# Second block's modulation vectors: 96 weight tiles multiplied on TensorE during the spreading of the gates, instead of 160 row products on VectorE during the expert stage

## The reference, cut to what matters

```python
def modulation(cond, w_mod, b_mod):
    return jnp.split(jax.nn.silu(cond) @ w_mod + b_mod, 6, axis=-1)   # 1024 -> 6 x 1024, for 2 layers, cond = c and c_ctx

def peer(...):                       # first block
    ... idx, gate = the 16 chosen experts of each head and their softmax
    act = gelu(einsum('td,thkd->thk', hb, u_tab[idx])) * gate
    return einsum('thk,thkd->td', act, v_tab[idx])
```

## Time and profile before

| | |
|---|---|
| median of 3 runs | 4271.44 us (4268.54 to 4271.95) |
| profiled execution | 4277.81 us, span of the trace 4276.0 us |
| spreading loop | 1098 to 1289 us of the span |
| expert stage | 1289 to about 2350 us of the span |
| instructions on DVE for this modulation | 160 of 1.22 us |

### The profile page before, as it was taken

How to read it: one execution, slowest core, us unless ns; L and a number is a source line. 1 busy time by engine, 2 the same in 40 slices (tenths; PEclk the granted TensorE clock), 3 DMA queues, 4 the chain that set the end, 5 groups by cost and what they waited for, 6 DMA issues and landing times.

```text
span 4276.0 us, 50001 instructions
## 1 busy us (share of the span) xinstructions
PE 3972.7 (93%) x19979; PEld 3173.8 (74%) x19979; DVE 2581.3 (60%) x4442; ACT 1424.2 (33%) x2405; POOL 1699.5 (40%) x1029
## 2 busy tenths in 40 slices
PE   7888999999778999999999799889999989889998
PEld 4768755448667888888988666778888868656886
DVE  5687655438995899999887436444434430645334
ACT  4212211113683333333333336532222131533222
POOL 3246433124894444434444320033222354444443
PEclk9998999999889999999999899999999989999999
DMA  7110310142237999989997100012122112002331
GB/s 260 65 35 2 118 47 25 64 159 91 107 143 269 332 326 332 333 319 338 358 330 267 63 20 16 16 45 74 60 64 60 55 50 66 9 26 80 97 94 50
DMA packets 191332, 562.86 MB, mean 132 GB/s; under 512 B 16283, under 2 KB 66651, under 8 KB 188540
## 3 DMA queue, kind: packets, MB, share of 16 engines
q1 hardware_dynamic: 151100, 405.83, 27.1%
q0 software_dynamic: 40000, 153.84, 10.2%
HBM read 530.24 MB, written 29.36 MB: 131 GB/s over the span
## 4 chain that ended last, share of the span: by engine, by line
PE 54%; DVE 16%; issue 4%; POOL 4%; ACT 4%; DMA 1%; DVEq 0%; POOLq 0%; ACTq 0%
PE psum L271 14%; PE psum L273 14%; PE psum L272 14%; PE psum L277 11%; DVE pair L261 4%; DVE selrow L1952 3%; DVE junk L1974 2%; POOL o L1858 1%; PE psum L372 1%; DVE tok L1962 1%; DMA selrow<-peerrow,hiU 1%; DVE Al L1943 1%; ACT Ah L2032 1%; POOL Pe L2811 1%; DVE psum L1941 1%
## 5 line engine op out<-in xcount | busy, mean ns | idle before, releaser
L250 POOL TENSOR_TENSOR pair<-raw_ring,pair 128x1024 fp32r<-128x1024 f32 x263 | 645.5, 2461 | 1266.9 <-ACT pair L240 1214.0
L240 ACT CAST pair<-raw_ring 128x1024 fp32r<-128x1024 f32 x502 | 513.6, 1048 | 403.8 <-PE psum L273 369.0
L271 PE MATMUL psum<-pfh,pair 128*128 128x384 f32 (+1 forms) x1152 | 401.2, 348 | 22.4 <-DVE Al L1943 9.6
L273 PE MATMUL psum<-pfh,pair 128*128 128x384 f32 (+1 forms) x1152 | 396.7, 344 | 0.0
L272 PE MATMUL psum<-pfl,pair 128*128 128x384 f32 (+1 forms) x1152 | 396.3, 344 | 0.0
L271 PE MATMUL psum<-ffh,pair 128*128 128x512 f32 (+1 forms) x1056 | 379.8, 360 | 16.9 <-DVE ffl L2173 16.0
L272 PE MATMUL psum<-ffl,pair 128*128 128x512 f32 (+1 forms) x1056 | 379.3, 359 | 0.0
L273 PE MATMUL psum<-ffh,pair 128*128 128x512 f32 (+1 forms) x1056 | 379.3, 359 | 0.0
L2080 POOL DMA_INDIRECT selrow<-peerv,hiU x128 | 238.2, 1861 | 295.0 <-DVE tok L1962 255.5
L2080 POOL DMA_INDIRECT selrow<-peerrow,hiU x128 | 217.0, 1695 | 288.7 <-DVE hiF L1952 263.8
L271 PE MATMUL psum<-pair,Ah 128*128 128x512 f32 x768 | 305.5, 398 | 9.3 <-DVE pair L261 7.6
(11 more groups left out here) (644 smaller groups left out, 9068.7 us busy)
## 6 DMA issues: line engine op xcount, KB each, us to landing
raw_ring<-wmod SPq DMA_DIRECT2D x144, 512.0 KB
raw_ring<-peeru SPq DMA_DIRECT2D x128, 512.0 KB
raw_ring<-peerv SPq DMA_DIRECT2D x128, 512.0 KB
raw_ring<-win SPq DMA_DIRECT2D x48, 512.0 KB
gates<-stage SPq DMA_DIRECT2D x12, 2048.0 KB, 7.2
Gb<-gates SPq DMA_DIRECT2D x32, 768.0 KB, 9.3
raw_ring<-wgate SPq DMA_DIRECT2D x44, 512.0 KB
raw_ring<-wup SPq DMA_DIRECT2D x44, 512.0 KB
```

The costliest lines, as they stand in the source:

```text
L240: ac.e.copy(self.pair(t)[0], k.R.of(t)).then_inc(*k.A.up("hi", t))
L250: po.e.tensor_tensor(lo, k.R.of(t), hi.bitcast(F), ALU.subtract).then_inc(*k.G.up("lo", t))
L271: e.matmul(out, w[0], x[0], start=first, stop=False, skip_group_check=True)
L273: return e.matmul(out, w[1], x[0], start=False, stop=last, skip_group_check=True)
```

## The change

The product is done on PE, in the spreading loop. `w_mod` is laid out untransposed in tiles, so that tile t holds the eight 128-row blocks of 128 output columns. `modulated(t)` multiplies each block (moving, 128 columns) with a stationary 128 x 32 matrix of the conditions, silu(c) and silu(c_ctx) in its first two columns and zeros elsewhere. The eight products go in turn to four column positions of the array, that is to PSUM partitions 0, 32, 64 and 96, each position summing two. When four tiles are in a bank, ACT copies it to SBUF (`copied`), PE multiplies it with a 0/1 matrix `sel4` that adds the four positions and turns the result (`turned`), and ACT copies eight columns into `mods2`. Eight tiles are done ahead of the loop, and tile u+8 after unit u. The spread results now have four PSUM banks instead of six, the modulation two. The ring's order is changed: the 96 `wmod2` tiles stand after U9 (with U10, U11 and U12 between them), and U13 and all that follows stands after them. SP's loads between the gate writes are changed too. `deal()` charges ACT 0.2 more per unit, and so hands 201 `o1` to POOL, 111 to ACT, 72 to DVE. In the expert stage `mods`, the loads of the condition rows and their silu are gone; two additions of the bias stand at its start.

```diff
@@ tensor_route
+    def modulated(t):
+        if t % 4 == 0:
+            B.take(("mod2", t // 4), 1, PAIR)
+            pe.wait_ge(B.free(("mod2", t // 4)), A.at("cond2"))
+        o = slice(128 * (t % 4), 128 * (t % 4) + 128)
+        w = k.R.of(("wmod2", t))
+        pe.wait_ge(k.R.at(("wmod2", t)))
+        for q in range(8):
+            r = slice(32 * (q % 4), 32 * (q % 4) + 32)
+            i = mm(e, B.of(("mod2", t // 4))[r, o], k.cond2[:, q, :], w[:, 128 * q:128 * q + 128], q < 4, q > 3)
+        i.then_inc(*P.up("mod2", t))
+        k.R.over(("wmod2", t), P.now())
+    def turned(g):
+        pe.wait_ge(A.at("mrow2", g), G.at("sel4"))
+        for c in range(4):
+            i = mm(e, B.of(("mod2", g))[:, 2 * c:2 * c + 2], k.mrow2[g % 2][:, 128 * c:128 * c + 128], k.sel4)
+        i.then_inc(*P.up("modT2", g))
+    for t in range(8):
+        modulated(t)
+    turned(0)
+    turned(1)
     choose(0)
     for u in range(SPREADS):
-        bank = B.take(("sp", u), 1, SIX)
+        bank = B.take(("sp", u), 1, FOUR)
...
+        if u + 8 < 96:
+            modulated(u + 8)
+        if u % 4 == 2 and 2 <= (u + 2) // 4 < 24:
+            turned((u + 2) // 4)
@@ deal
-        load["scalar"] += 0.58
+        load["scalar"] += 0.58 + 0.2
@@ scalar_route
+    ac.wait_ge(k.G.at("cond2"))
+    e.activation(k.cond2[:, :, 0:2], v3(k.vec["c2"], 2), AF.Silu).then_inc(*A.up("cond2"))
...
+    def copied(g):
+        ac.wait_ge(P.at("mod2", 4 * g + 3), P.at("modT2", g - 2) if g > 1 else None)
+        e.copy(k.mrow2[g % 2], B.of(("mod2", g))).then_inc(*A.up("mrow2", g))
+    def turned(g):
+        i, j = g // 12, 4 * (g % 12)
+        ac.wait_ge(P.at("modT2", g))
+        e.copy(k.mods2[i][:, j:j + 4, :], v3(B.of(("mod2", g))[:, 0:8], 2)).then_inc(*A.up("modT2", g))
+        B.over(("mod2", g), A.now())
+...
         if u > 1:
             spread(u - 2)
+        if u % 4 == 1 and 2 <= (u + 3) // 4 < 24:
+            copied((u + 3) // 4)
+        if u % 4 == 3 and 2 <= (u + 1) // 4 < 24:
+            turned((u + 1) // 4)
@@ vector_experts
+    for i in range(2):
+        e.tensor_tensor(k.mods2[i], k.mods2[i], bc(...bmod2...), ALU.add).then_inc(*V.up("mods2", i))
-            if 0 <= t - MODS < 98:
-                mods(t - MODS)
@@ sync_program
-    R.load(sp, ("U", FIRST + 7))
     for ch in range(CHUNKS):
+        R.load(sp, ("wmod2", min(8 * ch + 18, 95)))
         sp.wait_ge(A.at("sp", 8 * ch + 7))
         e.dma_start(gd[ch], k.stage[ch % 2]).then_inc(*k.stl[ch % 2].up())
-        if ch == 0:
-            R.load(sp, ("U", AHEAD - 1))
-        if ch == 9:
-            R.load(sp, ("V", 1))
     R.load(sp, ("V", 3))
```

More of the change, by code:

```diff
@@ L1497, in lay_peer @@
     k.Gb = [m.take("Gb", 4 * DENSE) for _ in range(2)]
-    both = m.at
-    k.cb2 = [m.take("crow", 1024) for _ in range(2)]
-    k.junk = m.take("junk", 1024)
-    m.at = both
     k.tok = v3(m.take("tok", 4096), 1024)
@@ L1818, in scalar_route @@
         B.over(("ht", hf), A.now())
+    def copied(g):
[6 more added lines that the diff above has]
+        B.over(("mod2", g), A.now())
+    for g in range(2):
+        copied(g)
+    for g in range(2):
+        turned(g)
     choose(0)
@@ L1860, in pool_route @@
     G.name("end", "route")
-NG, MODS = 64, 16
+NG = 64
 def ups(gi):
@@ L3592, in load_order @@
         use(("wq", n))
-    for n in range(AHEAD):
+    for n in range(FIRST):
+        use(("U", n))
+    for t in range(96):
+        if t - 8 in BESIDE:
+            use(("U", BESIDE[t - 8]))
+        raw(("wmod2", t), d["wmod2"][t])
+    for n in range(FIRST + len(BESIDE), AHEAD):
         use(("U", n))
@@ L3687, in sync_program @@
         if t > 0:
[L3688 to L3691 removed]
+            due = W.when[("U", t + 1)] if t > 113 else [n for v in range(t) for n in W.when[("V", v)]]
+            R.load(sp, due[-1] if due else None)
             sp.wait_ge(V.at("act", t))
```

58 lines of the change are left out of this document (18 added, 40 removed).

## The result

| | before | after |
|---|---|---|
| median | 4269.99 us (4267.96 to 4271.95, 4 runs) | 4324.01 us (4321.00 to 4325.87, 4 runs) |
| ratio | | 1.0122 [1.0108, 1.0136] |
| profiled execution, span | 4277.81, 4276.0 us | 4325.87, 4324.1 us |

The direction was right, and the time lies inside the range of 4260 to 4325, but the forecast of +24 us was less than half of the +54. I split both spans at four marks: the last product of the query scores (`kt,qs`), the first and the last copy of `stage`, the last multiplication by `Al` (the end of the expert stage).

The account below looks back on a forecast made before the run. PE bounds the expert stage; in the loop four engines stand close together. Ahead 1, loop 4 + 24 + 10 = 38, expert stage's start 1, expert stage -16: +24 us, median 4295, range 4260 to 4325.

Parts of the forecast that it names:

- What bounds the kernel, and the expert stage: Expert stage: PE bounds it, with 18.2 us lost beside busy DVE and DMA engines; 16 us come back, bounds 8 and 19.
- The start of the expert stage: Start of the expert stage: six tiles load behind the last gate write, mostly covered; costs 1 us, bounds 0 and 6.
- The price of a tile: Spreading loop, on PE: a tile's 16 passes run four abreast, 0.43 us plus 0.2 for mode changes, 0.63 us.
- The two waits: Spreading loop: PE waits for tiles behind gate writes, 24 us (0 to 47); ACT waits for `turned`, 10 us (0 to 15).
- the loop's engines: Spreading loop: the new division of `o1` and ACT's copies add work to POOL, DVE and ACT; 4 us on the loop.
- the loop would be 215 to 240 us long: Sign in the trace after: the spreading loop takes 215 to 240 us rather than 191.
- Ahead of the loop: Before the spreading loop: ACT's exponential stands behind both groups' copies; costs 1 us, bounds 0 and 3.
- only two column positions: Rival, spreading loop: only two positions run abreast, a tile costs 0.43 us more on PE; 4313 us, chance 0.15.
- none: Rival, spreading loop: no positions run abreast or issue limits, a tile costs 1.9 us on PE; 4338 us, chance 0.07.
- The buffers swallow it: Rival, spreading loop: buffers absorb tile waits and handshake, the loop costs only its engines' 4 us; 4261 us, chance 0.17.
- the case in which it comes out even: Rival between swallowed and forecast, spreading loop: half the waits remain; about 4272 us, chance 0.13.
- the change does not do what it says: Rival, expert stage: its losses were not DVE's or the DMA's, so nothing returns; 4311 us, no chance given.

Follow-up runs that it names:

- e14: The changed kernel with the 16 condition columns loaded into a free stretch of cand, so other buffers lie as in the kernel before; ratio 1.0144.
- e7: The kernel before with the modulation's 160 DVE products out of the expert stage and its 96 loads kept; ratio 0.9947.
- e8: The kernel before with the modulation's 96 loads out of the expert stage and the 160 products kept, made on the condition rows; ratio 0.9999.
- e4: The kernel before with both the modulation's 160 DVE products and its 96 loads out of the expert stage; ratio 0.9963.
- e3: The changed kernel with ACT's small copy one unit later and SP loading four tiles further before each gate write; ratio 1.0039.
- e2: The changed kernel with SP loading tiles up to 8ch+22 instead of 8ch+18 before a gate write; ratio 1.0039.
- e5: e3 with each modulation tile in the loop loading only 128 columns (64 KB), used by all eight products; ratio 1.0019.
- e6: e3 with one product for a tile instead of eight, from the ninth tile on; ratio 1.0037.
- e9: e3 with U8, U9 and U10 three tiles earlier in the order of the ring's loads; ratio 1.0040.
- e17: The kernel before with the turn of the six PSUM banks moved on by three behind the loop; ratio 1.0027.
- e12: The kernel before with 16 unused columns more among the vector constants, so the buffers behind them lie 64 bytes further; ratio 0.9987.

## Why the forecast was half of the result

**What bounds the kernel, and the expert stage: right.** The term was -16 us, bounds 8 and 19. At equal places of the buffers it is -16.4 (e14's 1052.4 us against 1068.8). e7 and e8 show that of the two causes it named (DVE from 93 to 70%, the loads' share) only the first counts. Of the -13.3 us in the trace of after, the other 3 are the 64 bytes; the kernels with the new places and nothing of this work on DVE scatter from 1055.4 to 1058.8. One reading on the way was wrong: from 2000 us on not 56 products were still to come but 29, and only one for each tile (L1974 has ended):

```profile
L1976 DVE CUSTOM_DVE_ANT_0 raw_ring<-raw_ring,crow 128x1024 f32<-128x1024 f32 x29 | 35.3, 1217 | 0.0
```

So the full window there was weaker evidence that the products don't bound PE than it seemed.

**The start of the expert stage: right.** The term was 1 us; e14's expert stage, with six tiles loaded behind the last write, is 0.3 us longer than that of e4, which has neither products nor tiles.

**The price of a tile: right.** 0.63 us forecast, 0.57 measured at the full clock and 0.65 on average, four positions abreast. The Trainium skill ("TensorE: Matmul & The Clock Gate", Part 3) has 2.38 times for three positions. Here 96 passes at four positions took 2.83 us; less the 0.27 us that one pass takes by itself that is 0.027 us from start to start, where the whole array has 0.107 to 0.11: the trace shows some 4 times for four, and no run has three. The drain at a change of mode ("TensorEngine Tiling", Tiling Modes) agrees with 0.57 us in the loop against 0.43 from tile to tile in a row (16 x 0.027).

**The two waits: right in sum, partly by luck.** Terms: 24 us (half of 47) for the tiles and 10 for `turned`, 34 together; e3, with both edits, takes 33.5 us from the loop. The parts did not come as reckoned. PE waited for tiles 30.7 us and not 47, and "I take half" is not what happened: e2 took all but 1.8 us of these waits away and shortened the loop by 30.0, in part through the clock, which the prediction did not price. The wait for `turned` is worth 14.2 us alone and 3.5 once the tile waits are gone. Its term counted 2.6 us of PE's work against 1.9 of ACT's; it left out that in the two units with `turned` and a projection of U another 4.4 us stand ahead, and that each tile wait is handed to ACT through it.

**The step that failed: the loop's engines, "That is 4 us on the loop".** With both waits gone e3's loop is still 25.7 us longer than before. The division of `o1` is right (POOL's work +3.7 us, e3); what was put at nothing are three other things. PE's own work: "PE needs 1.75 us of a unit's 1.99. It fits". The sum prices every pass at the full clock and leaves the three projections of U out; e5 shows up to 1.99 us of PE a unit, and e6, with one product for eight, takes 7.6 us off the loop. The bytes: worked out at "16.2 us for a chunk, against 15.9", and then not added; e5 gives them 10.2 us. And POOL's wait for the rounded U, which comes later when the ring is full of tiles: 12 us in e3, of which an earlier place in the ring (e9) gives 4 back, and 6.8 us of the loop. How the three share the 25.7 us is open, as they overlap and no kernel has all three edits. So the loop was 59 us longer instead of 38, and the sentence that the loop would be 215 to 240 us long was missed by 6.

**Ahead of the loop: 1 us forecast, 3.5 measured**, above the bound of 3. The chain named (tiles 7 and 8, copy, `turned`, exponential) is the one in the trace. e5 shows that it takes the loads to make it late.

**What no step looked at.** Behind the expert stage the prediction had nothing. In fact +11.5 us lie there from the banks (e17), some 9 us come back there from the 64 bytes (e12: -5.5 in all, after +1.0 and +2.3 further ahead), and where the difference would be +2.7 the trace shows -2.2. Single profiles scatter that much there: 1907.9 to 1919.6 us in four kernels that don't differ behind the expert stage (before, e4, e7, e8). The two nearly cancel, so a total alone would have shown neither.

Of the rivals, "only two column positions" (4313) and "none" (4338) fell with the price of a tile. "The buffers swallow it", and the case in which it comes out even, fell with e2; "the change does not do what it says" (4311) fell with e7. That 4324 lies inside the range is luck: its upper part was there for two positions abreast, and what filled it is the engines' term. The upper bounds of both waits would have given 4323, but the waits were not at their bounds.

## What to carry to other kernels

Before work is put on an engine with idle time in a tight loop, add up all it must do in a unit, at the clock that its rows show, and compare that with the pace: here PE went from 75% busy to needing up to the whole of the old pace (e5), and what the loop waited for changed from POOL to PE and its loads. Where several engines have little slack, don't take half of a wait as absorbed: 30.0 us came back for 30.7 of waits, and 19.3 for 22.2, the clock's part included. An account of work and waits of the tight engine says where to try; only runs say what a part is worth. When an edit changes how many buffers, banks or bytes are handed out, compare the waits of the untouched stages too: here an allocation pointer moved 11.5 us and 64 bytes some 5, where the expert stage had 16 to give back, and with the pointer restored and half of the modulation moved the idea wins 0.5%.

## What the runs showed of the hardware

The place of SBUF buffers changes PE's rate at an unchanged granted clock of 1.00. Moved by 64 bytes, passes of 384 columns went from 504 to 500 records per 100 us of a mixed stretch, and passes of 512 columns in the last layer from 0.233 to 0.226 us (e12). Which operand's place does it was not tried.

Four column positions run some 4 times as fast as the whole array on passes of 128 columns. The loads of 50 MB beside a stage at a DMA share of 0.92 cost PE nothing as long as DVE held it back (e8), while seven eighths of the same bytes in a loop with 2 MB writes between them cost 10 us (e5).

Around each of PE's eight waits for a tile, 3.0 to 4.8 us long, the granted clock was 1.2 GHz for 3.4 to 6.9 us; with the waits gone the loop's granted clock was 0.95 instead of 0.88 (e2).
